# A two-layer encoder with routed experts: the first expert's rows by one-hot products, and identity products in three waits of TensorE

## What is computed

```python
scores = jax.nn.sigmoid(hf @ router_w)            # hf: 512 x 1024, router_w: 1024 x 16
biased = scores + router_bias
...                                               # best of 4 groups, then the top 2 experts in it
order = jnp.argsort(e_flat)                       # tokens sorted by expert
dest = pstart[e_sorted] + (jnp.arange(n_assign) - start[e_sorted])
slot_tok = jnp.full((cap,), T, jnp.int32).at[dest].set(tok_flat[order])
xs = hpad[slot_tok].reshape(n_blocks, DISPATCH_BLOCK, D)   # blocks of 128 rows, one expert each

def expert_block(args):
    xb, e = args
    return (jax.nn.silu(xb @ w_gate[e]) * (xb @ w_up[e])) @ w_down[e]
```

## Time and profile before

| | us |
|---|---|
| median of 3 runs | 1440.48 |
| lowest and highest run | 1439.84, 1441.86 |
| the profiled execution, its time | 1440.28 |
| the profiled execution, its span | 1438.5 |

### The profile page before, as it was taken

How to read it: one execution, slowest core, us unless ns; L and a number is a source line. 1 busy time by engine, 2 the same in 40 slices (tenths; PEclk the granted TensorE clock), 3 DMA queues, 4 the chain that set the end, 5 groups by cost and what they waited for, 6 DMA issues and landing times.

```text
span 1438.5 us, 14181 instructions
## 1 busy us (share of the span) xinstructions
PE 1267.1 (88%) x4821; PEld 813.9 (57%) x4821; DVE 945.9 (66%) x1336; ACT 592.0 (41%) x774; POOL 169.3 (12%) x177
## 2 busy tenths in 40 slices
PE   2979899948999999983899999999489999999881
PEld 2434344546666667741788854467466666667430
DVE  8468985566777777713866588856667777777114
ACT  3246200335555555502422157734255555554001
POOL 6100000010000000002000047710110000000002
PEclk9999999959999999997899999999599999999996
DMA  9984575047999999883375230023679999998445
GB/s 354 375 283 124 198 256 212 30 146 273 372 363 369 373 372 375 307 334 122 127 282 185 88 117 1 1 74 127 241 289 374 377 366 365 378 363 310 146 181 190
DMA packets 79615, 353.12 MB, mean 245 GB/s; under 512 B 12696, under 2 KB 12880, under 8 KB 70608
## 3 DMA queue, kind: packets, MB, share of 16 engines
q1 hardware_dynamic: 67680, 327.28, 61.7%
q0 software_dynamic: 8352, 20.46, 3.9%
q10 hardware_dynamic: 3536, 4.79, 0.9%
HBM read 334.15 MB, written 28.31 MB: 252 GB/s over the span
## 4 chain that ended last, share of the span: by engine, by line
PE 74%; DVE 12%; SPq 5%; DMA 4%; ACT 2%; issue 2%; POOL 1%; DVEq 0%; ACTq 0%; POOLq 0%
PE ps L1771 24%; PE ps L1782 17%; PE ps L1870 8%; PE ps L1691 4%; PE ps L1762 3%; PE ps L1658 3%; PE ps L1698 2%; PE ps L1757 2%; DVE scratch L974 2%; PE ps L1914 2%; PE ps L1942 2%; SPq L398 2%; PE ps L1928 2%; DMA mod_ring<-in_mod_w_dram 1%; PE ps L1621 1%
## 5 line engine op out<-in xcount | busy, mean ns | idle before, releaser
L1782 PE MATMUL ps<-slab_ring,scratch 128*128 128x512 f32 x560 | 246.5, 593 | 3.4 <-ACT scratch L882 2.1
L1771 PE MATMUL ps<-slab_ring_r,gate_rows_r 128*128 128x512 f32 x512 | 202.4, 395 | 0.0
L1782 PEld LDWEIGHTS ps<-slab_ring,scratch 128*128 128x128 f32 x560 | 105.8, 190 | 124.2 <-issue 117.3
L1377 DVE TENSOR_TENSOR slab_ring_r<-slab_ring,h_t_r 128x2048 fp32r<-128x2048 f32 x64 | 143.9, 2287 | 17.2 <-ACT h_t_r L804 17.1
L1658 PE MATMUL ps<-h_t,slab_ring 128*128 128x512 f32 x320 | 141.2, 600 | 0.0
L1870 PE MATMUL ps<-slab_ring_r 128*128 128x512 f32 x384 | 121.2, 397 | 2.7 <-DVE h_t_r L1031 2.7
L1771 PE MATMUL ps<-h_t_r,gate_rows_r 128*128 128x512 f32 x256 | 106.4, 415 | 14.8 <-DVE scratch_r L1407 7.6
L804 ACT ACTIVATE h_t_r<-slab_ring 128x2048 fp32r<-128x2048 f32 x64 | 118.6, 1901 | 0.0
L1771 PEld LDWEIGHTS ps<-slab_ring_r,gate_rows_r 128*128 128x128 f32 x512 | 98.4, 192 | 19.4 <-issue 0.5
L1658 PEld LDWEIGHTS ps<-h_t,slab_ring 128*128 128x128 f32 x320 | 61.8, 194 | 77.8 <-issue 77.2
L833 ACT ACTIVATE scratch<-ps,mod_ab 128x128 f32<-128x128 f32 x128 | 48.1, 456 | 136.0 <-PE ps L1757 136.0
(11 more groups left out here) (318 smaller groups left out, 2065.2 us busy)
## 6 DMA issues: line engine op xcount, KB each, us to landing
slab_ring<-in_expert_w_gate_dram SPq DMA_DIRECT2D x35, 2048.0 KB, 10.0
slab_ring<-in_expert_w_up_dram SPq DMA_DIRECT2D x35, 2048.0 KB, 10.4
slab_ring<-in_expert_w_down_dram SPq DMA_DIRECT2D x35, 2048.0 KB, 10.4
mod_ring<-in_mod_w_dram SPq DMA_DIRECT2D x48, 512.0 KB, 4.6
y_rows<-scratch SPq DMA_DIRECT2D x35, 512.0 KB, 10.8
slab_ring<-in_mod_w_dram SPq DMA_DIRECT2D x32, 512.0 KB, 4.6
slab_ring<-in_w_qkv_dram SPq DMA_DIRECT2D x6, 2048.0 KB, 11.3
slab_ring<-in_w_in_ab_dram SPq DMA_DIRECT2D x5, 2048.0 KB, 18.0
```

The lines of the kernel that those rows point to most:

```text
L1377: tt_(rest, w, top.bitcast(F32), ALU.subtract).then_inc(low_ready[c], 1)
L1771: ins = pe.matmul(ps[:, bank, :], x, w, start=(kt == 0 and i == 0), stop=(kt == KT - 1 and i == 2))
L1782: ins = pe.matmul(ps[:, 5 + h, :], hidT[:, f, :], w[:, 2 * f + h, :], start=(f == 0), stop=(f == FT - 1))
```

## The change

Expert 0's rows are no longer gathered. `first_hot` is a one-hot matrix already, so TensorE multiplies the normalised rows in SBUF by it: for each of the eight chunks four products (one for each token tile) that add up in banks 4 and 5 of PSUM, which gives the 128 rows already turned. This is in plain float32 (32 products of 128 x 128 by 128 columns). With it go the four products with the token numbers, DVE's two instructions behind them, expert 0's gather and its `turn_xs`. Banks 4 and 5 are read by ACT and DVE in place of 0 and 1.

`find_slots`, the last two instructions of `route`, moves on DVE behind the eviction of expert 0's rows. Bank 3 replaces bank 2 for the sum it reads.

`keep_clock(n)` issues n products of the identity by itself (128 x 128 by 128 columns, float32) into bank 7, which nothing reads. It stands at three places: 19 behind the last router product, 4 behind the rank products, 8 behind the products of `route`.

```diff
-            gather_first(0, xs_filled[0])
-            gp.wait_ge(slots_ready, 2 * l + 2)
             gather_first(1, xs_filled[1])
...
             tt_(first_hot, p_id[:, :].unsqueeze(1).to_broadcast([P, TT, P]), first_rank[:, :].unsqueeze(2).to_broadcast([P, TT, P]), ALU.is_equal).then_inc(place_ready, 1)
-            v.wait_ge(slots_summed, 2 * l + 1)
-            found = ps[:, 2, 0:1]
-            link(ts(empty[:, 0:1], found, 0.0, float(NO_TOKEN), ALU.is_equal, ALU.mult))
-            stt(slot_tok[:, 0:1], found, -1.0, empty[:, 0:1], ALU.add, ALU.add).then_inc(slots_ready, 1)
-            v.wait_ge(slots_ready, 2 * l + 1)
...
             xst(0, 0, True)
+            find_slots(l)
             step(0, 0, first=True)
...
+            def keep_clock(products):
+                for _ in range(products):
+                    pe.matmul(ps[:, 7, 0:P], ident[:, :], ident[:, :], start=True, stop=True)
...
             turn_x(s, TT - 1)
             logits(TT - 1)
+            pe.wait_ge(ht_dve, TT * s + TT)
+            keep_clock(19)
             pe.wait_ge(hot_ready, TT * (l + 1))
...
             ins.then_inc(rank_ready, 1)
+            keep_clock(4)
             pe.wait_ge(place_ready, 2 * l + 1)
-            for t in range(TT):
-                ins = pe.matmul(ps[:, 2, 0:2], first_hot[:, t, :], tok_pair[:, t, :], start=(t == 0), stop=(t == TT - 1))
-            ins.then_inc(slots_summed, 1)
+            pe.wait_ge(xn_ready, TT * s + TT)
+            for kt in range(KT):
+                for t in range(TT):
+                    ins = pe.matmul(ps[:, FIRST_BANK + kt // 4, (kt % 4) * P:(kt % 4 + 1) * P], xnorm[s][:, t, kt:D:KT], first_hot[:, t, :], start=(t == 0), stop=(t == TT - 1))
+                if kt == 3:
+                    ins.then_inc(first_rows, 1)
+            ins.then_inc(first_rows, 1)
...
-            pe.wait_ge(xs_filled[0], (NE // 2) * l * 16 + 16)
-            turn_xs(0, xs_turned)
+            keep_clock(8)
+            pe.sem_inc(xs_turned, 1)
             step(0, 0, 0, first=1)
```

More of the change, by code:

```diff
@@ L149, in build @@
     rw_scaled, rw_shift = (R[:, 12, i * P:(i + 1) * P].rearrange("p (k e) -> p k e", e=NE) for i in range(2))
-    first_hot = R_r[:, 12, :].rearrange("p (t n) -> p t n", n=P)
+    first_hot = R[:, 12, :].rearrange("p (t n) -> p t n", n=P)
     comb = [[XN[:, t, :] for t in range(TT)],
@@ L181, in build @@
     shift_row = small("router_shift_row", [P, NE])
-    tok_pair = small("token_id_pair", [P, TT, 2], F32R)
     first_rank = small("first_rank", [P, TT])
@@ L254, in build @@
     xs_turned, xst_act, xst_dve = sem("xs_turned"), sem("xst_act"), sem("xst_dve")
+    first_rows = sem("first_rows")
     high_ready, low_ready = [sem("gate_high"), sem("up_high")], [sem("gate_low"), sem("up_low")]
@@ L338, in build @@
     LAST = 4 * 7 + AV_LAG
+    FIRST_BANK, SLOT_BANK = 4, 3
     QK_BANK = [0, 1, 2, 3, 4, 5, 0, 1] + [2, 4, 5, 6, 7, 6, 7, 6]
@@ L632, in gathers @@
             link(gp.memset(R[:, 0:4, :], 0.0))
-            gp.wait_ge(slots_ready, 2 * l + 1)
+            gp.wait_ge(slots_ready, l + 1)
             gp.wait_ge(xn_stored, 16 * TT * (l + 1))
@@ L830, in xst @@
                     act.wait_ge(route_ready, l + 1)
-                act.wait_ge(xs_turned, e + (e0 + 1))
+                if first and not par:
+                    act.wait_ge(first_rows, 2 * l + 1)
+                else:
+                    act.wait_ge(xs_turned, e + (e0 + 1))
+                bank = FIRST_BANK if first and not par else 0
                 for kt in range(4):
-                    ins = act.activation(xsT[par][:, kt, :], ps[:, 0, kt * P:(kt + 1) * P], ACT.Identity, bias=AB[:, s, 1, kt:kt + 1], scale=AB[:, s, 0, kt:kt + 1])
+                    ins = act.activation(xsT[par][:, kt, :], ps[:, bank, kt * P:(kt + 1) * P], ACT.Identity, bias=AB[:, s, 1, kt:kt + 1], scale=AB[:, s, 0, kt:kt + 1])
                 ins.then_inc(xst_act, 1)
@@ L1238, in _ @@
         n = TT * NE
-        link(v.tensor_copy(tok_pair[:, :, :], tok1[:, :].unsqueeze(2).to_broadcast([P, TT, 2])))
         sc, bia, o1, o2, t0, t1, t2, t3 = (rt[:, i * n:(i + 1) * n] for i in range(8))
@@ L1322, in route, with find_slots @@
             v.wait_ge(place_ready, 2 * l + 2)
-            v.wait_ge(slots_summed, 2 * l + 2)
-            slots = ps[:, 2, 1:WIDE]
+        def find_slots(l):
+            v.wait_ge(slots_summed, l + 1)
+            slots = ps[:, SLOT_BANK, 1:WIDE]
             link(ts(empty[:, 1:WIDE], slots, 0.0, float(NO_TOKEN), ALU.is_equal, ALU.mult))
             stt(slot_tok[:, 1:WIDE], slots, -1.0, empty[:, 1:WIDE], ALU.add, ALU.add).then_inc(slots_ready, 1)
-            v.wait_ge(slots_ready, 2 * l + 2)
+            v.wait_ge(slots_ready, l + 1)
         def route_rest(l):
@@ L1398, in xst @@
                     v.wait_ge(up_done, e + (e0 - 1))
-                v.wait_ge(xs_turned, e + (e0 + 1))
+                bank = 1
+                if first and not par:
+                    bank = FIRST_BANK + 1
+                    v.wait_ge(first_rows, 2 * l + 2)
+                else:
+                    v.wait_ge(xs_turned, e + (e0 + 1))
                 for kt in range(4, KT):
-                    ins = ts(xsT[par][:, kt, :], ps[:, 1, (kt - 4) * P:(kt - 3) * P], AB[:, s, 0, kt:kt + 1], AB[:, s, 1, kt:kt + 1], ALU.mult, ALU.add)
+                    ins = ts(xsT[par][:, kt, :], ps[:, bank, (kt - 4) * P:(kt - 3) * P], AB[:, s, 0, kt:kt + 1], AB[:, s, 1, kt:kt + 1], ALU.mult, ALU.add)
                 ins.then_inc(xst_turned, 1)
@@ L1743, in experts @@
             ins.then_inc(rank_ready, 1)
+            keep_clock(4)
             pe.wait_ge(place_ready, 2 * l + 1)
-            for t in range(TT):
-                ins = pe.matmul(ps[:, 2, 0:2], first_hot[:, t, :], tok_pair[:, t, :], start=(t == 0), stop=(t == TT - 1))
-            ins.then_inc(slots_summed, 1)
+            pe.wait_ge(xn_ready, TT * s + TT)
[5 more added lines that the diff above has]
+            ins.then_inc(first_rows, 1)
             pe.wait_ge(place_ready, 2 * l + 2)
             for i in range(2 * TT):
-                ins = pe.matmul(ps[:, 2, 0:WIDE], place_hot[:, i, :], block_tok[:, i, :], start=(i == 0), stop=(i == 2 * TT - 1))
+                ins = pe.matmul(ps[:, SLOT_BANK, 0:WIDE], place_hot[:, i, :], block_tok[:, i, :], start=(i == 0), stop=(i == 2 * TT - 1))
             ins.then_inc(slots_summed, 1)
@@ L1810, in step @@
                 if not last:
-                    pe.wait_ge(xs_filled[1 - par], (turn + par) * 16 + (16 + (NE // 2) * l * 16))
+                    if par == 0:
+                        pe.wait_ge(xs_filled[1], turn * 16 + (16 + (NE // 2) * l * 16))
+                    else:
+                        pe.wait_ge(xs_filled[0], turn * 16 + (16 + (NE // 2 - 1) * l * 16))
                     turn_xs(1 - par, xs_turned)
```

## The result

| | before | after |
|---|---|---|
| median, us (20 runs each) | 1441.18 | 1443.31 |
| lowest and highest run, us | 1439.11, 1443.33 | 1440.50, 1449.01 |
| ratio to before, 95% interval | | 1.0021 (1.0014 to 1.0028) |
| the profiled execution: time, span, us | 1440.28, 1438.5 | 1440.50, 1438.7 |

The changed kernel is 0.2% slower, some 3 us by the ratio, where 12.9 us of gain were forecast. Its profiled execution is the lowest of its runs, only 0.2 us longer than the profiled one of before; so the rows show less of the loss than the medians do.

The account below looks back on a forecast made before the run. TensorE's work plus its standstills and half-clock stretches bound the kernel. Faster expert-stage entries gain 5.39 us in layer 0 and 7.49 in layer 1, 12.9 in all: 1440.28 becomes 1427.4 us, range 1422.5 to 1437.

Parts of the forecast that it names:

- the third of the sum: One-hot products at the expert stage's entry: 32 products, 64 records of 0.111 us, 7.10 us in all.
- the fall of the clock behind the second step: Slow clock after TensorE's standstill before the second step might not occur: up to 3.4 us less in two layers.
- The upper bound of the price: Identity and one-hot records at 0.126 instead of 0.111 us would cost 3.1 us, giving 1430.5 us.
- the sign itself: Among the one-hot products, 64 records of 0.2 us would show the forecast wrong.
- Step 1: 19 identity products behind the router products: clock rises after 4.65 us; they end 1.02 us after the choice is there.
- Step 2: Rank products to `first_hot` 1.67 us as before; TensorE begins the one-hot products 0.05 us later.
- Step 4: From the turned rows to the first gate product: 3.16 us, plus 0.11 us of handover.
- Step 5: Before the gate products only 0.8 us of standstill; clock stays up, 24 gate products take 5.47 us instead of 7.99.
- The covers: Second step still starts 10.30 us behind the gate products; expert 1's rows, wanted at 318.74, cost nothing landing by 322.6.
- The clock that does not rise: Rival, chance 0.11: identity, one-hot and gate products all run at half clock; 1451.2 us, slower.
- the one that rises late: Rival, chance 0.10: the clock rises only among the one-hot products; 1436.8 us.
- The second: Rival, chance 0.09: identity and one-hot records cost 0.218 us, 1450.4 us; the change loses from 0.174 a record on.

## Why the prediction was wrong

**The step that failed is the third of the sum: 64 records of 0.111 us.** They took 15.26 us to the next row's start in each layer, 0.238 a record, in place of 7.10. The price had come from the turns with the identity, whose data lie 32 bytes apart too and which cost 0.111 all the same, and from the gate products, whose weights are neighbours; neither is a plain float32 product with spread weights. Put into the sum, 2 x (15.26 - 7.10) = 16.3 us turn 1427.4 into 1443.7 us; the measured median is 1443.31. That the two are so close is in part luck. The sum starts from the profiled execution of before, and that of the kernel after took 1440.50, 3.2 us less than 1443.7. Some 1.7 of these are the fall of the clock behind the second step, by the prediction's own price, which in layer 0 did not come (0.57 before); the kernel after:

```profile
337.00:340.00 3.00, 2.90 (x13) 2.35 (x14) 2.81 (x3) 0.00 (x0) 0.00 (x0) 1.00 0.98 399
```

Where the other 1.5 lie these rows don't tell.

The upper bound of the price, 0.126, was made for something that might come on top of the overlap, and did not look at how the weights lie. The prediction had named the sign itself: 64 records of 0.2 us.

The other steps held, in layer 0 of the kernel after unless said:

- **Step 1, the 19 identity products.** The clock rises among them, as forecast. The choice is there at 300.43 + 0.18 = 300.61 and the ranks start at 300.77, so they run over by 0.16 us; in layer 1 (choice at 1015.71, ranks at 1016.68) by 0.97. Forecast: 1.02 in both.
- **Step 2.** Ranks to one-hot products 302.45 - 300.77 = 1.68 us; forecast 1.72.
- **Step 4.** From DVE's start at 318.06 to the gate products 3.19 us; forecast 3.16.
- **Step 5.** The clock stays up through the 0.62 us of standstill, and 24 gate products take some 5.5 us; forecast 5.47.
- **The covers.** The second step starts 15.86 us behind the first gate product, 5.5 and the carried 10.3. Expert 1's rows come late for their turn, by 0.84 us, inside the 3.9 us of slack that the prediction left. In layer 0 the clock does not fall before the second step, where TensorE stands 2.65 us; in layer 1, after 3.42 us, the cold first record (0.77) shows that it does. The wait alone does not settle it: in the version with the rows laid out by chunks the same step is cold behind the same 2.65 us (0.77 at 330.13).

**The rivals.** The clock that does not rise, and the one that rises late, fell with the stretches above. The second, load and streaming one after the other, was near in its number (0.218) and wrong in its mechanism: identity products, and one-hot products with neighbouring weights, run 0.112 us apart at full clock, so the two lie beside each other there. The rule of the Trainium skill that the prediction cited for it ("TensorE: Matmul & The Clock Gate", "The mechanism") does not hold in these rows, if only another row group counts; the same section also names loads into a background weight buffer, which the prediction left out, and no run here tells which it is. The rival's point of decision, 0.174 us a record, was right as arithmetic: with 0.238 for 64 of the 102 records and 0.111 for the others the mean is 0.19, and the change loses.

## What to carry to other kernels

Price a new product by the row that shares its number format and the layout of its weights, not only its shape: here a strided float32 weight slice doubled the cost, and a line of the old kernel with the very same load durations had shown it, at full clock too. Identity products in a wait can pay for themselves, but only where the clock they raise still holds when the dear products begin. And when a change moves no time, look for the row that has grown: the mechanism may be worth its forecast once that one row is mended.

## What the runs showed of the hardware

- A plain float32 product with 128 weight columns costs 0.112 to 0.118 us a record at full clock with the columns 4 or 8 bytes apart and 0.233 to 0.238 with 16 or 32 bytes; at 32 bytes it keeps that pace at half clock (64 records in 15.53 us, begun at 0.50, against 15.50). A turn whose data lie 32 bytes apart costs 0.111 all the same. Why it differs, these runs don't tell.
- POOL took longer to issue expert 1's gather, and its copy of the next indices. In the kernel after, layer 0:

```profile
322.39 2.35 POOL L638 DMA_INDIRECT scratch<-xn_rows,slot_token  x1 [26.01 <-DVE slot_token L1326]
324.75 1.28 POOL L643 COPY gather_idx<-slot_token 128x1 int32 x1
```

  Before it was 1.01 us. The moved gather now falls beside DVE's low parts (321.49 to 325.99); that this is the cause is only argued. It cost nothing: the second step starts 15.86 us behind the first gate product there, and 15.87 in layer 1, where the turn did not wait for the rows.
